# First feed-forward of a two-block transformer kernel: the output product as seven half-size block products in place of eight

## The reference, cut to what matters

```
def swiglu(x, w_in, w_out):
    gate, up = jnp.split(x @ w_in, 2, axis=-1)
    return (jax.nn.silu(gate) * up) @ w_out

def ffn_half(s, shift, scale, gate, g_pre, g_post, w_in, w_out):
    h = swiglu(modulate(rmsnorm(s, g_pre), shift, scale), w_in, w_out)
    return s + 0.5 * gate * rmsnorm(h, g_post)
```

## Time and profile before

| | |
|---|---|
| median of 3 runs | 1926.42 us (1924.99 to 1927.2) |
| profiled execution | 1927.17 us, span of its instructions 1925.4 us |
| TensorE busy | 1732.5 us, 90% of the span |
| VectorE busy | 874.4 us, 45% |
| ScalarE / GpSimd busy | 308.7 us, 16% / 164.6 us, 9% |
| mean granted TensorE clock | 0.955 |
| the stage of the change | 322.4 to 475.4 us |

### The profile page before, as it was taken

One profiled execution on the slowest core, in us unless ns is written; L12 is line 12 of the kernel. 1 busy time (PEld: TensorE's weight loads), 2 busy tenths in 40 slices (PEclk: granted clock), 3 DMA queues, 4 the chain that ended last, 5 costly groups with the idle time before them and its releaser, 6 DMA issues.

```text
span 1925.4 us, 28951 instructions
## 1 busy us (share of the span) xinstructions
PE 1732.5 (90%) x11848; PEld 1371.0 (71%) x11848; DVE 874.4 (45%) x1760; ACT 308.7 (16%) x697; POOL 164.6 (9%) x159
## 2 busy tenths in 40 slices
PE   8999999999999999999999999999999765655656
PEld 3888888888888989679999998877778221221214
DVE  5766666965466466644676136743433000000001
ACT  2200000010210002422111114322323000000001
POOL 3000000010133310001000002612001000000000
PEclk9999999999999999999999999989999987787878
DMA  9433334965442214126545863101379999999997
GB/s 374 148 130 129 128 130 160 346 244 197 153 153 88 88 45 154 66 87 220 195 171 179 291 213 130 45 24 46 131 279 377 407 430 433 430 432 433 430 432 302
DMA packets 47043, 426.04 MB, mean 221 GB/s; under 512 B 5364, under 2 KB 5973, under 8 KB 16093
## 3 DMA queue, kind: packets, MB, share of 16 engines
q1 hardware_dynamic: 37296, 386.97, 51.7%
q10 hardware_dynamic: 9644, 37.59, 5.4%
HBM read 423.49 MB, written 1.05 MB: 220 GB/s over the span
## 4 chain that ended last, share of the span: by engine, by line
PE 71%; DMA 18%; DVE 5%; issue 2%; ACT 2%; POOL 1%; POOLq 0%; SPq 0%; ACTq 0%; DVEq 0%
PE bank L1027 26%; DMA arena<-experts_ring_dram 18%; PE bank L1161 13%; PE bank L1211 8%; PE bank L1595 3%; PE bank L1310 3%; PE bank L1308 3%; PE bank L1664 2%; PE bank L1969 2%; PE bank L1488 1%; ACT arena L2254 1%; DVE arena L3232 1%; DVE tiny L3034 1%; PE bank L1363 1%; PE bank L1353 1%
## 5 line engine op out<-in xcount | busy, mean ns | idle before, releaser
L1027 PE MATMUL bank<-arena 128*128 128x256 f32 (+1 forms) x2912 | 507.5, 336 | 0.5 <-ACT arena L2471 0.5
L1027 PEld LDWEIGHTS bank<-arena 128*128 128x128 f32 x2912 | 459.2, 191 | 46.6 <-issue 1.8
L1969 PE MATMUL bank<-arena 128*32 128x512 f32 x1400 | 213.2, 763 | 145.3 <-DMA arena<-experts_ring_dram 145.3
L1969 PEld LDWEIGHTS bank<-arena 128*32 128x32 f32 x1400 | 58.1, 135 | 293.5 <-issue 293.3
L1161 PE MATMUL bank<-arena 128*128 128x256 f32 x880 | 193.9, 379 | 0.0
L1161 PEld LDWEIGHTS bank<-arena 128*128 128x128 f32 x880 | 167.1, 190 | 23.1 <-issue 0.5
L1211 PE MATMUL bank<-arena 128*128 128x128 f32 x1456 | 162.9, 275 | 0.0
L1211 PEld LDWEIGHTS bank<-arena 128*128 128x128 f32 x1456 | 162.8, 192 | 0.1
L3426 DVE TENSOR_TENSOR arena<-arena,bank 128x512 f32<-128x512 f32 x8 | 5.5, 688 | 240.8 <-PE bank L1969 240.8
L905 POOL TENSOR_TENSOR rstd<-sq 128x128 f32<-128x128 f32 (+2 forms) x9 | 6.7, 740 | 971.6 <-ACT sq L2091 971.6
L2732 DVE SCALAR_TENSOR_TENSOR arena<-arena 128x1024 f32<-128x1024 f32 x56 | 68.3, 1221 | 0.0
(11 more groups left out here) (500 smaller groups left out, 2233.8 us busy)
## 6 DMA issues: line engine op xcount, KB each, us to landing
arena<-dense_dram SPq DMA_DIRECT2D x167, 1024.0 KB, 4.9
arena<-experts_ring_dram SPq DMA_DIRECT2D x41, 4096.0 KB, 26.9
arena<-ada_rest_dram ACTq DMA_DIRECT2D x56, 512.0 KB, 5.5
arena<-experts_dram SPq DMA_DIRECT2D x18, 1024.0 KB, 8.8
arena<-ada_head_dram SPq DMA_DIRECT2D x8, 1024.0 KB, 23.6
arena<-experts_dram SPq DMA_DIRECT2D x10, 512.0 KB, 9.4
arena<-tokens_dram ACTq DMA_DIRECT2D x1, 2048.0 KB, 20.7
arena<-experts_ring_dram SPq DMA_DIRECT2D x1, 2048.0 KB, 23.5
```

The lines of the kernel that those rows point to most:

```text
L1027: ins = mm(out, lhsT=w, rhs=rhs(k), start=k == 0, stop=k == k_tiles - 1)
L1969: ins = mm(ps[banks[half]][32 * e:32 * e + 32, :], lhsT=lhs[:, 2 * kp + par, CAP * e:CAP * e + CAP], rhs=slab[e][par][:, half * 512:half * ...
```

## The change

The output product for one token set is `w_out` (transposed) times `hid1`. It is cut into pairs p of output tiles, two halves of 11 hidden tiles, and two halves of 128 tokens. In place of eight block products of 11 matmuls x 128 tokens it makes seven (Strassen's scheme in Winograd's form). So for each token set r and each of four pairs p there are 7 x 11 = 77 matmuls of 128 tokens, 616 in all, where there were 352 of 256 tokens.

- **PE**: a pair's slab of weights holds four hidden tiles of each of the four blocks (the third slab three), so three slabs make one pair and the seven accumulators, four in one bank and three in another, stay open over them. The stage now has 24 slabs in place of 22.
- **POOL** makes four weight sums for each slab (24 x 4 operations, 128 x 512, in the third slab of a pair 128 x 384), at most two slabs ahead of PE. One sum is written into the slab itself. Norm 2's sums follow the 18th slab.
- **DVE** makes four token sums for each of three steps and each token set (24 operations) and joins the seven products in five operations for each pair, in two parts, which also empty the banks. ACT copies one product and takes the squares from `y1`. The context's token sums are written over the hidden layer of `x`, so the first of them waits until PE has ended the `x` half.
- **Modulation tiles**: the counts stay, 28 and 8. In the `x` half seven go ahead of each pair's joins; in the context half four stand after each of the first two pairs' joins, ahead of norm 2's normalisation. Their scratch moves from `fh` to a part of `y1` and, later, of `h1`. `fh` now holds weight sums.
- Norm 3's root and the context's residual come one z tile later.

```diff
+OUT_HALF, OUT_STEPS = FT // 2, 3
+OUT_SUMMED = KD * OUT_STEPS
...
-DENSE = [("ffn1_in", FT), ("ffn1_out", 22), ("z", 12), ("q", 4), ("k", 4), ("v", 4), ("gates", 7),
+DENSE = [("ffn1_in", FT), ("ffn1_out", 24), ("z", 12), ("q", 4), ("k", 4), ("v", 4), ("gates", 7),
...
+        def out_hidden(r, c):
+            a = slice(out_step(c)[0], out_step(c)[-1] + 1)
+            b = slice(a.start + OUT_HALF, a.stop + OUT_HALF)
+            return [hid1[:, ks, T * r + o:T * r + o + P] for ks in (a, b) for o in (0, P)]
+
+        def out_tokens(r, c):
+            n = len(out_step(c))
+            if r:
+                a, b = out_hidden(0, c)[0:2], out_hidden(0, c)[2:4]
+                return a[0], a[1], b[0], b[1]
+            at = [page(6 + 0.75 * c, 2 * n * P)[:, m * n * P:m * n * P + n * P].rearrange("p (k n) -> p k n", n=P) for m in range(2)]
+            fourth = page(6 + 0.75 * c + 0.5, n * P, P) if c < OUT_STEPS - 1 else page(13.5, n * P, P)
+            return at[0], at[1], out_hidden(0, c)[1], fourth
...
-            sum_squares(2, T)
+            pool.wait_ge(in_hid, FT)
+            for n in range(OUT_SUMMED):
+                slab, s, made, nk = SLAB0["ffn1_out"] + n, n % 2, 4 * FT + 4 * n, len(out_step(n % OUT_STEPS))
+                w = ring[slab % RING]
+                w0, w1, w2, w3 = (w[:, m * nk:m * nk + nk, :] for m in range(4))
+                s1, s2, s4 = (v_[s][:, 0:nk, :] for v_ in (out_s1, out_s2, out_s4))
+                pool.wait_ge(slab_loaded[slab % RING], 16 * (slab // RING + 1))
+                if n > 1:
+                    pool.wait_ge(ws_used, FT + n - 1)
+                nc.gpsimd.tensor_tensor(s1, w2, w3, add).then_inc(ws_ready, 1)
+                pool.wait_ge(ws_ready, made + 1)
+                nc.gpsimd.tensor_tensor(s2, s1, w0, sub).then_inc(ws_ready, 1)
+                nc.gpsimd.tensor_tensor(w2, w0, w2, sub).then_inc(ws_ready, 1)
+                pool.wait_ge(ws_ready, made + 2)
+                nc.gpsimd.tensor_tensor(s4, w1, s2, sub).then_inc(ws_ready, 1)
+                if n == OUT_SUMMED // 2 + 5:
+                    sum_squares(2, T)
...
+            def out_region(b, o, lhs, rhs, n, start, stop, started=None):
+
+                for k in range(n):
+                    ins = mm(ps[b][:, o:o + P], lhsT=lhs[:, k, :], rhs=rhs[:, k, :], start=start and k == 0, stop=stop and k == n - 1)
+                    if k == 0 and started is not None:
+                        ins.then_inc(started, 1)
+                return ins
+
+            def out_products(r, p, c):
+                n, nk, (a, b), use = 12 * r + 3 * p + c, len(out_step(c)), TWO_SETS[p % 2], 2 * r + p // 2
+                s, first, last = n % 2, c == 0, c == OUT_STEPS - 1
+                slot = st.slab % RING
+                assert st.slab == SLAB0["ffn1_out"] + n
+                w0, w1, w2, w3 = (ring[slot][:, m * nk:m * nk + nk, :] for m in range(4))
+                s1, s2, s4 = (v_[s] for v_ in (out_s1, out_s2, out_s4))
+                first_a, _, first_b, second_b = out_hidden(r, c)
+                t1, t2, t3, t4 = out_tokens(r, c)
+                pe.wait_ge(slab_loaded[slot], 16 * (st.slab // RING + 1))
+                st.slab += 1
+                if r == p == 0:
+                    pe.wait_ge(in_hid, OUT_HALF + out_step(c)[-1] + 1)
+                if first:
+                    take(pe, "ffn1_out", a, use)
+                out_region(a, 0, w0, first_a, nk, first, False, slab_started)
+                out_region(a, P, w1, first_b, nk, False, False)
+                pe.wait_ge(ot_ready, 12 * r + 4 * c + 2)
+                pe.wait_ge(ws_ready, 4 * FT + 4 * n + 2)
+                out_region(a, 2 * P, s2, t2, nk, False, False)
+                ins = out_region(a, 3 * P, s1, t1, nk, False, last)
+                if last:
+                    ins.then_inc(full[a], 1)
+                if first:
+                    take(pe, "ffn1_out", b, use)
+                pe.wait_ge(ot_ready, 12 * r + 4 * c + 4)
+                pe.wait_ge(ws_ready, 4 * FT + 4 * n + 4)
+                out_region(b, 0, s4, second_b, nk, first, False)
+                out_region(b, P, w2, t3, nk, False, False)
+                ins = out_region(b, 2 * P, w3, t4, nk, False, last, ws_used)
+                if last:
+                    ins.then_inc(full[b], 1)
...
-            for t in range(2 * KD):
-                take(pe, "ffn1_out", t % 4, t // 4)
-                product(ps[t % 4][:, 0:T], FT, lambda k: x_then_ctx(t, k), full[t % 4],
-                        arrived=None if t else last_hidden(in_hid))
-                first_norms(t)
+            for r in range(2):
+                for p in range(KD // 2):
+                    for c in range(OUT_STEPS):
+                        out_products(r, p, c)
+                        if (r, p, c) == (1, 0, 1):
+                            stat_of_sum(1, T)
+                        elif (r, p, c) == (1, 2, 1):
+                            stat_of_sum(2, T)
...
-            for t in range(KD):
-                leave("ffn1_out", 1, y1, t)
-                for n in range(4 * t, min(4 * t + 4, ADA_FIRST)):
-                    ada_load(n % ADA_TURN, 0, IN_TURNS + n // ADA_TURN)
-            leave("ffn1_out", 3, y1, 0, T)
+            def ada_late_load(n):
+                ada_load(n % ADA_TURN, 0, IN_TURNS + n // ADA_TURN)
+
+            def out_copy(r, p):
+                a = TWO_SETS[p % 2][0]
+                got(act, "ffn1_out", a, 2 * r + p // 2)
+                A(y1[:, 2 * p + 1, T * r + P:T * r + T], ps[a][:, 0:P], ACT.Copy).then_inc(in_copied, 1)
+
+            def out_squares(r, p):
+                evacuated(act, "ffn1_out", TWO_SETS[p % 2][1], 2 * r + p // 2)
+                for t in range(2 * p, 2 * p + 2):
+                    square(3 if r else 1, t, y1[:, t, T * r:T * r + T], T)
+
+            for p in range(KD // 2):
+                for n in range(ADA_FIRST // 4 * p, ADA_FIRST // 4 * p + ADA_FIRST // 4):
+                    ada_late_load(n)
+                out_copy(0, p)
+                out_squares(0, p)
...
-            def ada_late(n):
+            def ada_late(n, scratch):
                 turn = IN_TURNS + n // ADA_TURN
-                ada_tile(n % ADA_TURN, 0, turn, fh)
+                ada_tile(n % ADA_TURN, 0, turn, scratch)
                 if n % ADA_TURN == ADA_TURN - 1:
                     ada_bias(0, turn)
-            for j in range(KD):
-                for n in range(4 * j, min(4 * j + 4, ADA_FIRST)):
-                    ada_late(n)
-                if j:
-                    add_square(1, j, T)
+
+            def out_token_sums(r, c):
+                a1, a2, b1, b2 = out_hidden(r, c)
+                t1, t2, t3, t4 = out_tokens(r, c)
+                made = 12 * r + 4 * c
+                tt_(t1, a2, a1, sub).then_inc(ot_ready, 1)
+                dve.wait_ge(ot_ready, made + 1)
+                tt_(t2, b2, t1, sub).then_inc(ot_ready, 1)
+                tt_(t3, b2, a2, sub).then_inc(ot_ready, 1)
+                dve.wait_ge(ot_ready, made + 2)
+                tt_(t4, b1, t2, sub).then_inc(ot_ready, 1)
+
+            def out_join_first(r, p):
+                a, use, y = TWO_SETS[p % 2][0], 2 * r + p // 2, out_view(r, p)
+                dve.wait_ge(in_copied, FT + 4 * r + p + 1)
+                do(tt_(y[:, :, 0, :], ps[a][:, P:3 * P].rearrange("p (a n) -> p a n", n=P), y[:, 1:2, 1, :].to_broadcast([P, 2, P]), add))
+                settle()
+                tt_(y[:, 1, 1, :], y[:, 1, 0, :], ps[a][:, 3 * P:4 * P], add).then_inc(evac[a], 1)
+
+            def out_join_second(r, p):
+                (a, b), use, y = TWO_SETS[p % 2], 2 * r + p // 2, out_view(r, p)
+                got(dve, "ffn1_out", b, use)
+                evacuated(dve, "ffn1_out", a, use)
+                do(tt_(y[:, 0, 1, :], y[:, 1, 1, :], ps[b][:, 0:P], add))
+                settle()
+                do(tt_(y[:, 1, :, :], y[:, 1, :, :], ps[b][:, P:2 * P].unsqueeze(1).to_broadcast([P, 2, P]), add))
+                settle()
+                tt_(y[:, 1, 0, :], y[:, 1, 0, :], ps[b][:, 2 * P:3 * P], add).then_inc(evac[b], 1)
+
+            def out_view(r, p):
+                return y1[:, 2 * p:2 * p + 2, T * r:T * r + T].rearrange("p o (h n) -> p o h n", n=P)
+
+            def out_sums(r, p):
+                for t in range(max(2 * p, 1), 2 * p + 2):
+                    add_square(3 if r else 1, t, T)
+
+            dve.wait_ge(in_hid, FT)
+            for c_ in range(OUT_STEPS):
+                out_token_sums(0, c_)
+            for p in range(KD // 2):
+                for n in range(ADA_FIRST // 4 * p, ADA_FIRST // 4 * p + ADA_FIRST // 4):
+                    ada_late(n, y1[:, 0:4, T:2 * T])
+                if p:
+                    out_sums(0, p - 1)
+                out_join_first(0, p)
+                if p == KD // 2 - 1:
+                    got(dve, "ffn1_out", 3, 1)
+                    out_token_sums(1, 0)
+                out_join_second(0, p)
```

(39 more changed lines are left out.)

58 lines of the change are left out of this document (32 added, 26 removed).

## The result

| | before | change |
|---|---|---|
| median of 4 runs | 1926.14 us (1924.99 to 1927.2) | 1998.84 us (1996.34 to 2000.32) |
| profiled execution, span | 1927.17 us, 1925.4 us | 1999.37 us, 1997.5 us |
| TensorE / VectorE / GpSimd busy | 90% / 45% / 9% | 87% / 49% / 17% |
| mean granted TensorE clock | 0.955 | 0.935 |

The ratio is 1.0376, interval 1.0358 to 1.0394: slower by 72.2 us in the profiled executions. 1993.0 us was predicted, with a range of 1960 to 2008 us.

A forecast was written before the change was run, and what follows sets the result against it. PE was taken to bound the stage, with DVE nearly full; after the change PE waits for DVE, held by POOL. Context half's end +62.1 us and stage z +4.0 us make 66.1 us on 1927.17 us: 1993 us, range 1960 to 2008 us.

The forecast's parts named there:

- DVE's own list: DVE's work from 323.8 us to the context's first token sums: 86.6 us, so 410.4 us at the earliest.
- POOL's hold: POOL's 56 sums before the context's token sums delay DVE by 46 us, moving those sums to 456.4 us.
- The price of 1.06 us: Delay to DVE for each POOL operation of 512 columns, whatever DVE's width; 0.80 us for 384 columns.
- the credit for joins and pauses: POOL work beside 6.8 us of joins and some 2 us of DVE pauses is free, leaving 46 of 55.2 us.
- The context half: After the token sums: 67.0 us PE work, 4 clock, 9.2 POOL sums, 0.9 norm 1; ends at 537.5 us, +62.1 us.
- The clock behind the long wait: Context half: PE's clock drops after standing still some 20 us, costing 4 us, bounds 0 and 5.
- Stage z: Its first tile waits for a late DVE join that empties bank 0: +4.0 us, between 0 and 6.
- The accumulating form is not held: Rival: POOL does not delay the modulation tiles' accumulating passes; +17 us, 1944 us; chance 0.08.
- Nothing is shared: Rival: POOL and DVE do not delay each other; stage ends at 478.3 us, total 1930 us; chance 0.04.
- Faster: Rival: DVE has the context's token sums ready when PE asks, before 407.5 us; 1913 us; chance 0.03.
- Slower still: Rival: PE's pauses at slabs lower the clock, half speed for some 15 us more; 2010 us; chance 0.08.
- the 14.3 us: PE's predicted gain over the stage if it never waits: 137.6 us of matmuls in place of 151.9 us.

The follow-up runs named there:

- write-only run: The change, with each of POOL's 96 weight sums in the stage replaced by three memsets of about the same length that read nothing in SBUF: 1938.49 us.
- run with neither reads nor passes: The change, with POOL's sums replaced by instructions that only write and the 72 passes over the modulation tiles left out: 1922.72 us.
- no-passes run: The change, with the 72 passes of the 36 modulation tiles in this stage left out and POOL's sums all kept: 1930.82 us.

## Why the prediction was right

**DVE's own list.** Predicted: token sums at 410.4 us with nothing held. The write-only run has PE going on at 414.99 us. Of the 4.6 us, 2.9 us are modulation tiles that landed late there (DVE idle 1.06, 1.50 and 0.32 us, released by their DMA; the change has no such wait), and 1.1 us are two waits for ACT's copy ahead of a first join, which I had costed at nothing. PE came to this point late as well, at 397.0 us for 393.2 us, so that its wait of 17.95 us for 17 us is closer than either end.

**POOL's hold.** Predicted: 46 us. Measured: 460.86 - (414.99 - 2.9) = 48.8 us. The price of 1.06 us, taken from instructions of 256 and 512 columns, held for a pass of 1024 columns that accumulates, and so did the three quarters for a POOL sum of 384 columns: two of these start 1.94 us apart beside passes (363.74 and 365.68 us), 0.80 us more than 1.14 us. What was too large is the credit for joins and pauses. The biases, which I had counted among the pauses, take their turn with POOL as well: one of eight columns, 0.17 us alone, took 1.10 us in four of the seven cases. PE's wait before the third region was 17.8 us (about 20 predicted), and PE stood still 56.0 us in the `x` half (some 60). For banks it waited three times, not two: 4.7 and 15.1 us at the third and fourth pair, and 10.6 us at the context's first; this last one cost nothing, as the token sums came later still. POOL was busy for 171 us in the stage (over 120).

**The context half.** Predicted 81.1 us from the token sums to the end, measured 82.0 us (460.86 to 542.9). The terms: PE waits for POOL's sums 1.57 + 2.39 + 2.34 + 1.77 + 1.36 = 9.4 us, for 9.2. The clock behind the long wait (columns as in the stretches above):

```profile
455.00:461.00 6.00, 0.14 (x1) 0.15 (x1) 5.69 (x14) 0.28 (x1) 0.00 (x0) 0.50 0.69 227
461.00:466.00 5.00, 5.00 (x30) 5.00 (x31) 4.88 (x10) 2.01 (x3) 0.00 (x0) 0.64 0.02 8
466.00:471.00 5.00, 5.00 (x48) 5.00 (x47) 4.88 (x6) 0.00 (x0) 4.10 (x4) 1.00 0.45 147
```

A share of 0.36 of 5 us is 1.8 us. A second dip, which I had not placed, comes in the middle of the half, behind PE's short waits (0.95 and 0.77 in two stretches of 6 us from 507 us): 1.7 us. Together 3.5 us, for 4. That this fits is in part luck: the 4 us were meant for the long wait alone, and the rows they came from the earlier trace rows stand behind a wait of PE of only 1.48 us, which ended at 1287.30 us. Norm 1's matmul did not wait; the 0.9 us for it are about the time of the half's two statistics matmuls, 0.43 us each. The terms as measured, 67.0 + 9.4 + 3.5 + 0.9 us, leave 1.2 us of the 82.0 us unplaced.

**Stage z.** Predicted +4.0 us by a late join. PE waits 2.2 us at its start (the view of the waits puts them to "issue"). The kernel has it wait there for the join that empties bank 0 (timeline of DVE):

```profile
543.42 0.94 DVE L2678 TENSOR_TENSOR sd<-sd,sq 128x256 f32<-128x256 f32 x2
544.28 0.42 DVE L3020 TENSOR_TENSOR arena<-bank,arena 128x256 f32<-128x256 f32 x1
544.73 0.29 DVE L3022 TENSOR_TENSOR arena<-arena,bank 128x128 f32<-128x128 f32 x1
```

It is over at 545.0 us and z begins at 545.12. The k and v products come another 1.8 us later than z's start does; the granted clock of 0.98 over 545 to 632 us is 1.7 us. The sum is right by luck: only half of it is the join; the other half is the clock, which I had not priced there.

**The sum.** 72.2 us for 66.1. The step that was under-sized is the time of the context's token sums: 460.9 us where it says 456.4 us. It holds 4.5 of the 6.1 us: 0.7 us is the stage beginning later (323.3 for 322.6 us), 1.1 us ACT, and the 2.8 us are the hold, whose credit for joins and pauses was too large. 0.9 us fell in the context half, and 0.7 us is left over behind it. The range was narrower than its own terms: 14 us for the price, 4 and 1 us for the clock, 4 and 2 us for z, added plainly, give 1971 to 2010 us, not 1974 to 2008 us. The measured time lies in both.

**The rivals.** "The accumulating form is not held" is refuted by the passes of 2.09 to 2.27 us. "Nothing is shared" is what the write-only run plays: 1938.5 us; the rival's 1930 us was 8.5 us too low. In the trace the stage ends at 487.45 us where the rival has 478.3 us. Of these 9.1 us, 4.6 us are the token sums (above), 3.1 us are the clock behind the wait (granted 0.50 and 0.89 in the stretches 415 to 420 and 420 to 425 us), which its sum left out, and 1.1 us are two waits for POOL. "Faster" wanted token sums by 407.5 us; they come at 415 us even without a hold. "Slower still" didn't come: the clock dipped in the context half but came back. The rule of the Trainium skill ("SBUF — State Buffer", section "Who interferes with whom"), that a DVE instruction with two SBUF inputs contends with a GpSimd instruction that reads SBUF and not with one that only writes it, agrees with this case for the accumulating form too: 2.27 us beside a reading POOL instruction, 1.22 us beside one that only writes.

**What stays open.** The seven products in the context half alone, where DVE had 34 us to spare before, were not tried. Half of the 14.3 us would be the most that they could bring, and the run with neither reads nor passes kept a third of the whole. Nor was another split of the tiles between the two halves tried, the plainest way to shorten DVE's list ahead of PE's wait. In the write-only run DVE is busy for 84.4 of 92.1 us up to the context's token sums, but for only 50.2 of 72.5 us behind them, so there was room for some tiles there. Whether PE's wait would go by this, with POOL's reads or without them, isn't shown.

## What to carry to other kernels

Fewer matmul cycles are paid for with sums on other engines. Add up the list of the engine that takes them up to the point at which PE waits, in program order, and compare it with PE's new and shorter time, since an average such as 45% busy hides a stage in which the engine is at 89%. Then look at where the operands of the two elementwise engines lie: here each POOL sum of 1.27 us that read SBUF beside DVE's two-operand passes added 1.06 us to DVE. A bank as operand (1955.2 us) or writes in place of reads (1938.5 us) took the hold away, but not the length of the list.

## What was not expected of the hardware

- A tiny instruction waits nearly as long as a large one: the bias of eight columns took 0.16 or 0.17 us alone and 1.10 or 1.11 us beside POOL, four times in the `x` half.
- The hold follows reading. POOL instructions that only write, three of them about as long together as a sum by itself, leave DVE's passes at 1.22 us, and DVE with one operand in a bank leaves POOL at 1.27 us.
- What a wait costs in clock is not one number. Behind the change's wait of 17.8 us the granted clock was 0.64 and then 1.00 in two stretches of 5 us, 1.8 us lost; behind the write-only run's wait of 17.95 us it was 0.50 and 0.89, 3.1 us lost; behind the no-passes run's wait of 5.7 us, 0.50 and 0.93 (405 to 415 us). It also fell to 0.77 for 6 us behind three stretches of 6 us in which PE was busy for 4.43, 3.61 and 3.66 us, as these rows from 495 us on show:

```profile
495.00:501.00 6.00, 4.43 (x40) 4.27 (x39) 5.69 (x10) 0.72 (x2) 5.92 (x4) 1.00 0.62 229
501.00:507.00 6.00, 3.61 (x33) 3.45 (x32) 5.90 (x7) 0.00 (x0) 5.92 (x4) 1.00 0.48 144
507.00:513.00 6.00, 3.66 (x31) 3.50 (x30) 5.90 (x5) 0.00 (x0) 6.00 (x4) 0.95 0.80 295
513.00:519.00 6.00, 6.00 (x42) 5.95 (x41) 5.76 (x12) 1.48 (x4) 5.92 (x5) 0.77 0.38 100
```
